# Final stage of a hybrid decoder step: PSUM as VectorE's work space, the norm's weights on GpSimd, the scaling on ScalarE

## The chip, the cores and the metric

The kernel runs on one core of one Trainium2 chip. The metric is device time in microseconds (us) of one execution; the median of 3 runs counts. A core has TensorE for matmuls (PE in the profile), VectorE (DVE), ScalarE (ACT), GpSimd (POOL) and SyncE (SP), which issues most DMAs. SBUF and PSUM are its two on-chip memories, both of 128 partitions; PSUM has 8 banks of 512 float32 per partition.

## The reference, cut to what matters

The reference is one layer of a decoder for 1024 prompt tokens and 8 sample tokens (D_MODEL 1024, float32): an mLSTM and a convolution, then a mixture of experts (top 2 of 32), a residual add and a final RMSNorm. The change is about the last lines only:

```
out = out + jnp.einsum('nef,efd->nd', hid * combine[:, sl, None], w_down[sl])   # two experts per token
...
x = x + g2[:, None] * moe
...
y_prompt = rms_norm(xp, final_g)
y_sample = rms_norm(xs, final_g)
```

`rms_norm` is `xf * rsqrt(mean(xf * xf) + EPS) * g`.

## The kernel before, in words

The 1032 tokens are 9 tiles: tiles 0 to 7 hold 128 prompt tokens each, tile 8 the 8 sample tokens. Each engine has its own program, and the order on an engine is written out by hand; between engines semaphores are waited on (`sem(name)` counters; a DMA adds 16). `chain(...)` on an engine makes its next instruction wait for the one just issued.

The experts run one after the other (32, and in this run 4 more passes for experts with more than 128 tokens; `nq` counts such groups of four). TensorE multiplies, ScalarE and VectorE split every float32 weight into a high and a low part (`ehi`, `elo`, `dhi`, `dlo`), GpSimd gathers tokens and scatters each expert's results to `ye_dram` (named `expert_results` in the trace), where row 2t+c is the c-th expert's result for token t. SP loads the weights of an expert into one of 4 slots of `eraw` and `draw`, as slots come free (`gu_ps` counts the gate-and-up products done). The residual stream lies in `x2_dram` (`x_scratch` in the trace).

The final stage begins when VectorE has seen all scatters land (`experts_done`, line 1383). Its buffers `xf` (residual), `y12` (the two expert results of each token) and `of` (output) lie where the expert weights were. `xf` and `y12` have FB = 4 places, `of` has 2, so a tile's loads wait for an earlier tile's place. For each tile:

- ScalarE, `weighted` (line 1189): first result times its weight, in place in `y12`.
- VectorE, lines 1399, 1400, 1402: second result times its weight plus the first; times `g2b` (the gate g2); plus the residual, into `xf`.
- ScalarE, lines 1200 to 1202: squares of `xf`, summed into `ssq`; logarithm; exponential, which gives 1/rms.
- VectorE, `scaled` (line 1391): `xf` times 1/rms times `fgb` (final_g), into `of`. It is issued one tile later, after the next tile's three passes.
- SP, `y_out` (line 1049): stores the tile. SP also loads: the first four residual tiles once the last expert's gate-and-up product is done (line 1027), the first four `y12` tiles after `experts_done`, and each later tile behind the store of the tile four before it.

Of the kernel before, what the change touches and what calls it, by code (L numbers as in the profile page):

```python
# [104 lines left out]
def build(nc, x_prompt, x_sample, c_prompt, c_sample, C0, n0, m0, cache, w_ada, b_ada, norm1_g, w_in,  # L105
# [10 lines left out]
    with ExitStack() as ctx:  # L116
        sems = {}

        def sem(name):
            if name not in sems:  # L120
                sems[name] = ctx.enter_context(nc.semaphore(name))
            return sems[name]

        def step(name):

            return sem("steps_" + STEP[name][0])
# [15 lines left out]
        def sb(scope, name, shape, dt=F32):  # L142
            return scope.enter_context(nc.sbuf_tensor(name, shape, dt))
# [851 lines left out]
        def moe_loads(sp):  # L995
            sp.wait_ge(sem("h2_ready"), NT)
            for e in range(NS):
                gate_up_load(sp, e, e, None)
                down_load(sp, e, e, None)
            sp.dma_start(fgb[:, :], final_g.rearrange("(o n) -> o n", o=1).broadcast_to([P, D])).then_inc(sem("fg_in"), 16)  # L1000
            for e in range(NS, NE):
                gate_up_load(sp, e, e % NS, e - NS + 1)
                if e > NS:
                    down_load(sp, e - 1, (e - 1) % NS, e - NS)
            down_load(sp, NE - 1, NS - 1, NE - NS)

            sp.wait_ge(step("nov_ready"), after("nov_ready"))
            nq = sp.value_load(nov[0:1, 0:1], min_val=0, max_val=MORE)
            with sp.Fori(QUADS, QUADS + MORE) as r:
                with sp.If(nq + QUADS > r):  # L1010
                    for half in range(2):
                        es = [sp.value_load(ovx[0:1, bass.ds(r * NS + (2 * half + b - NE), 1)], min_val=0, max_val=NE - 1)
                              for b in range(2)]
                        for b in range(2):
                            q = 2 * half + b
                            gate_up_load(sp, es[b], q, r * NS + (q - NS + 1))
                        for b in range(2):
                            q = 2 * half + b
# [12 lines left out]
            for t in range(NT + FB - 1):
                if t < NT:
                    b, m = t % FB, rows[t]
                    if t >= FB:
                        sp.wait_ge(sem("of_ready"), t - FB + 1)
                        x2_load(t)

                    sp.dma_start(y12[0:m, b, :, :].rearrange("p c n -> p (c n)"),
                                 ye_dram[2 * t * P:2 * (t * P + m), :].rearrange("(t c) n -> t (c n)", c=2))\
                      .then_inc(sem(f"y12_in{b}"), 16)  # L1040
                if t >= FB - 1:
                    y_out(sp, t - FB + 1)
            for s, v in (("out_done", 16 * 2), ("tails_out", 32), ("m_out", 32), ("c_out", 64), ("state_out", 32), ("x2_out1", 16 * 4),
                         ("h2_out", 16 * NT), ("y_out0", 16 * 5), ("y_out1", 16 * 4)):
                sp.wait_ge(sem(s), v)

        def y_out(sp, t):
            sp.wait_ge(sem("of_ready"), t + 1)
            sp.dma_start(y_d[t], of[0:rows[t], t % 2, :]).then_inc(sem(f"y_out{t % 2}"), 16)

        def moe_pool(pool, chain):
            pool.wait_ge(step("stage1_over"), after("stage1_over"))
# [44 lines left out]
                        late_scatter(r * NS + (q - LATE), (q - LATE) % 2, passes, r * 32 + 16 * ((q - LATE) // 2))  # L1097
            for q in range(LATE):
                late_scatter(nq * NS + (NE - LATE + q), (q - LATE) % 2, nq * (2 * NS) + 2 * q, nq * 32 + 16 * ((NE - LATE + q) // 2))

        def moe_act(act, chain):
            act.wait_ge(step("gmax_ready"), after("gmax_ready"))
# [82 lines left out]
            def weighted(t):  # L1185

                b, m = t % FB, rows[t]
                act.wait_ge(sem(f"y12_in{b}"), 16 * (t // FB + 1))
                act.activation(y12[0:m, b, 0, :], y12[0:m, b, 0, :], ACT.Copy, scale=wts[0:m, 0, t:t + 1])\
                   .then_inc(sem("ya_ready"), 1)  # L1190

            weighted(0)
            for t in range(NT):
                if t + 1 < NT:
                    weighted(t + 1)
                b, m = t % 2, rows[t]
                act.wait_ge(sem("xsum_ready"), t + 1)
                if t >= 2:
                    act.wait_ge(sem(f"y_out{b}"), 16 * (t // 2))
                chain(act.activation(of[0:m, b, :], xf[0:m, t % FB, :], ACT.Square, accum_out=ssq[0:m, b, 0:1]))  # L1200
                chain(act.activation(ssq[0:m, b, 1:2], ssq[0:m, b, 0:1], ACT.Ln, bias=epst[0:m, :], scale=1.0 / D))
                act.activation(ssq[0:m, b, 1:2], ssq[0:m, b, 1:2], ACT.Exp, scale=-0.5).then_inc(sem("rf_ready"), 1)

        def moe_dve(dve, chain):
            def signal(name):
# [181 lines left out]
            def scaled(t):

                m, b = rows[t], t % 2
                dve.wait_ge(sem("rf_ready"), t + 1)  # L1390
                dve.scalar_tensor_tensor(out=of[0:m, b, :], in0=xf[0:m, t % FB, :], scalar=ssq[0:m, b, 1:2], in1=fgb[0:m, :],  # L1391
                                         op0=ALU.mult, op1=ALU.mult).then_inc(sem("of_ready"), 1)


            for t in range(NT):
                b, m = t % FB, rows[t]
                dve.wait_ge(sem("ya_ready"), t + 1)
                ya, yb = y12[0:m, b, 0, :], y12[0:m, b, 1, :]
                chain(dve.scalar_tensor_tensor(out=ya, in0=yb, scalar=wts[0:m, 1, t:t + 1], in1=ya, op0=ALU.mult, op1=ALU.add))  # L1399
                chain(dve.tensor_tensor(ya, ya, g2b[0:m, t // NC_, :], ALU.mult))  # L1400
                dve.wait_ge(sem(f"xf_in{b}"), 16 * (t // FB + 1))
                dve.tensor_tensor(xf[0:m, b, :], xf[0:m, b, :], ya, ALU.add).then_inc(sem("xsum_ready"), 1)  # L1402
                if t:
                    scaled(t - 1)
            scaled(NT - 1)
# [644 lines left out]
```

## Time and profile before

| | us |
|---|---|
| median of 3 runs | 1085.94 (1085.92 to 1086.76) |
| profiled execution, its own time | 1092.49 |
| its span, first to last instruction | 1089.5 |
| busy in the span: TensorE / VectorE / ScalarE / GpSimd | 941.8 / 750.1 / 493.5 / 156.3 |
| `experts_done` in the span | 1035.97 |

Busy times are averages over stages with different limits. The change is read from the last stage alone, the stretch from 1035.97 to 1089.5, 53.5 us, in which TensorE does nothing. All times of day below count from the span's start.

### The profile page before, as it was taken

The numbers are of one execution on the slowest core, as the hardware profiler recorded it, in microseconds if no ns is written. First come the engines' busy times: TensorE is split into PE (matmuls) and PEld (weight loads), VectorE is DVE, ScalarE is ACT, GpSimd is POOL, SyncE is SP. The second block draws the span as 40 slices with busy tenths as digits, with TensorE's granted clock in tenths as the row PEclk, the third lists the DMA queues.
The fourth block names the chain that finished last, engine by engine and source line by source line (L and its number), as shares of the span: only waits on it lengthen the run. The fifth ranks groups of instructions, "written<-read, shape, count | busy, mean of one in ns | idle before, by whom it ended". The sixth has DMA issues, their size and how long they took to land. (4 is left out here: it accounts for less than half of the span.)

```text
span 1089.5 us, 12729 instructions
## 1 busy us (share of the span) xinstructions
PE 941.8 (86%) x4961; PEld 765.1 (70%) x4961; DVE 750.1 (69%) x939; ACT 493.5 (45%) x621; POOL 156.3 (14%) x120
## 2 busy tenths in 40 slices
PE   4599999989999989999999815899999999999700
PEld 2298979989999776666665314688888888888500
DVE  3441399969995343656445348799999999989478
ACT  4451212133121353333222204588888888888344
POOL 0100000000000000000000001133444444365200
PEclk9699999999999968899999956899999999999955
DMA  7963711102120160111141196489999999997276
GB/s 266 363 267 106 299 56 39 39 1 48 45 67 1 79 199 20 58 59 59 59 136 72 47 246 255 180 342 377 360 406 380 388 391 380 410 379 308 94 301 245
DMA packets 64775, 213.14 MB, mean 196 GB/s; under 512 B 13856, under 2 KB 34992, under 8 KB 46782
## 3 DMA queue, kind: packets, MB, share of 16 engines
q1 hardware_dynamic: 54350, 195.42, 47.9%
q0 software_dynamic: 10368, 16.93, 4.2%
q8 instruction: 39, 0.64, 0.2%
q14 instruction: 18, 0.15, 0.0%
HBM read 199.14 MB, written 34.49 MB: 214 GB/s over the span
## 5 line engine op out<-in xcount | busy, mean ns | idle before, releaser
L1220 DVE TENSOR_TENSOR elo<-eraw,ehi 128x2048 fp32r<-128x2048 f32 x72 | 161.4, 2283 | 0.0
L1846 DVE SCALAR_TENSOR_TENSOR z<-z,wdT 128x1024 f32<-128x1024 f32 x120 | 146.2, 1280 | 0.8
L1112 ACT ACTIVATE ehi<-eraw 128x2048 fp32r<-128x2048 f32 x72 | 133.6, 1907 | 1.9 <-issue 1.0
L1957 PE MATMUL ps<-hhi,whi 128*128 128x344 f32 x576 | 125.5, 327 | 6.4 <-ACT hhi L1690 3.6
L848 PE MATMUL ps<-wout,z 128*128 128x512 f32 (+1 forms) x288 | 127.6, 596 | 0.5 <-DVE z L688 0.5
L1957 PE MATMUL ps<-hhi,wlo 128*128 128x344 f32 x576 | 123.5, 323 | 0.0
L1957 PE MATMUL ps<-hlo,whi 128*128 128x344 f32 x576 | 122.9, 322 | 0.0
L1668 ACT ACTIVATE z<-ps 128x1032 f32<-128x1032 f32 x24 | 24.8, 1034 | 210.8 <-PE ps L1957 210.8
L1957 PEld LDWEIGHTS ps<-hhi,whi 128*128 128x128 f32 x576 | 98.6, 192 | 9.4 <-issue 9.3
L1957 PEld LDWEIGHTS ps<-hhi,wlo 128*128 128x128 f32 x576 | 98.7, 191 | 0.0
L1957 PEld LDWEIGHTS ps<-hlo,whi 128*128 128x128 f32 x576 | 97.2, 190 | 0.0
L848 PEld LDWEIGHTS ps<-wout,z 128*128 128x128 f32 (+1 forms) x288 | 50.7, 181 | 64.7 <-issue 64.0
L1819 DVE TENSOR_TENSOR wlo<-wraw,whi 128x1024 fp32r<-128x1024 f32 x22 | 26.9, 1225 | 83.7 <-ACT whi L1662 83.6
L1225 DVE TENSOR_TENSOR dlo<-draw,dhi 128x2048 fp32r<-128x2048 f32 x36 | 82.4, 2288 | 0.0
L1430 PE MATMUL ps<-ehi,xhi 128*128 128x512 f32 x288 | 77.4, 411 | 2.1 <-issue 2.1
L1063 POOL DMA_INDIRECT expert_results<-ysb,lists x27 | 72.5, 2684 | 34.6 <-ACT ysb L1138 34.6
L1430 PE MATMUL ps<-ehi,xlo 128*128 128x512 f32 x288 | 72.7, 395 | 0.0
L1430 PE MATMUL ps<-elo,xhi 128*128 128x512 f32 x288 | 71.1, 389 | 0.0
L1118 ACT ACTIVATE dhi<-draw 128x2048 fp32r<-128x2048 f32 x36 | 69.6, 1932 | 0.0
L1053 POOL IOTA ioti<- 128x128 int32 x1 | 0.2, 240 | 472.0 <-DVE marks L1207 472.0
L1344 DVE TENSOR_TENSOR xlo<-ps,xhi 128x1024 fp32r<-128x1024 f32 x36 | 44.1, 1225 | 30.2 <-ACT xhi L1122 30.2
L1430 PEld LDWEIGHTS ps<-ehi,xlo 128*128 128x128 f32 x288 | 55.4, 192 | 12.0
(368 smaller groups left out, 1489.7 us busy)
## 6 DMA issues: line engine op xcount, KB each, us to landing
eraw<-in_w_gate SPq DMA_DIRECT2D x36, 1024.0 KB, 11.5
eraw<-in_w_up SPq DMA_DIRECT2D x36, 1024.0 KB, 14.5
draw<-in_w_down SPq DMA_DIRECT2D x36, 1024.0 KB, 14.7
wada<-in_w_ada SPq DMA_DIRECT2D x24, 1024.0 KB, 10.5
wraw<-in_w_in SPq DMA_DIRECT2D x12, 1024.0 KB, 5.3
y<-expert_results SPq DMA_DIRECT2D x8, 1024.0 KB, 7.6
xt<-in_x_prompt SPq DMA_DIRECT2D x8, 512.0 KB, 6.2
wout<-in_w_out SPq DMA_DIRECT2D x2, 2048.0 KB, 10.0
```

Source lines behind the costliest of these rows:

```text
L848: mm = pe.matmul(ps[0:n, bank + a, :], lhs, wout[:, k, a * 512:(a + 1) * 512], start=(k == H), stop=(k == H - 1))
L1063: pool.indirect_dma_start(out=ye_dram, in_=ysb[:, b, :], in_offset=None, out_offset=bass.IndirectOffsetOnAxis(ap=at, axis=0), bounds_check ...
L1112: act.activation(ehi[:, s % 2, i, :, :], eraw[:, s, i, :, :], ACT.Copy).then_inc(sem("ehi_ready"), 1)
L1118: act.activation(dhi[:, s % 2, :, :], draw[:, s, :, :], ACT.Copy).then_inc(sem("dhi_ready"), 1)
L1220: dve.tensor_tensor(elo[:, s, i, :, :], eraw[:, s, i, :, :], ehi[:, s % 2, i, :, :].bitcast(F32), ALU.subtract)\
L1225: dve.tensor_tensor(dlo[:, s, :, :], draw[:, s, :, :], dhi[:, s % 2, :, :].bitcast(F32), ALU.subtract)\
L1344: dve.tensor_tensor(xlo[:, b, :, :], ps[:, 0:2, :].rearrange("p a (k n) -> p (a k) n", k=4), xhi[:, b, :, :].bitcast(F32), ALU.subtract).t ...
L1430: mm = pe.matmul(ps[:, 2, :].rearrange("p (i f) -> p i f", i=2), x[:, b, k, :], w[:, :, k, :], start=(i + k == 0), stop=(i == 2 and k == K ...
L1668: act.activation(z[:, j, PAD:ZW].rearrange("p (c n) -> p c n", c=3), ps[:, 3 * v:3 * v + 3, 0:TW], ACT.Sigmoid if GB0 <= j < Q0 or j >= O0 ...
L1819: dve.tensor_tensor(wlo[:, u, :, v * P:(v + 1) * P], wraw[:, u, :, v * P:(v + 1) * P], whi[:, v, :, :].bitcast(F32), ALU.subtract).then_in ...
L1846: dve.scalar_tensor_tensor(out=z[:, GB0 + b, PAD:SC], in0=z[:, U0 + b, w:w + T], scalar=wdT[:, b, w:w + 1], in1=z[:, GB0 + b, PAD:SC], op0 ...
L1957: mm = pe.matmul(ps[0:n, bank + c, 0:TW], w(k), h[:, k, c * TW:(c + 1) * TW], start=first, stop=last)
```

## The change

The final stage is written anew; the experts' arithmetic stays.

- ScalarE writes the weighted first result into PSUM instead of SBUF. VectorE's first two passes read and write it there, and the third adds it to the residual in SBUF. Four pairs of banks are used in turn.
- The product with `fgb` moves to GpSimd (`of` = `xf` times `fgb`), and the product with 1/rms to ScalarE, in place in `of`, one tile later. VectorE keeps both for the last tile only.
- `xf`, `y12` and `of` get a place for each tile, so no load or store waits for a place.
- The residual is loaded within the last experts: tiles 0 to 3, 4 to 7 and 8 when the first, second and third slot of the last group of experts are done with.
- The sample tile comes first (`FINAL`). Six loads bring `y12`: tile 8, tile 0, tile 1, then tiles 2 and 3, 4 and 5, 6 and 7 (`GROUP`).

```
-FB = 4
+FINAL = (8, 0, 1, 2, 3, 4, 5, 6, 7)
+GROUP = (1, 2, 3, 3, 4, 4, 5, 5, 0)
...
-        xf = sb(st3, "xf", [P, FB, D])
-        y12 = sb(st3, "y12", [P, FB, 2, D])
-        of = sb(st3, "of", [P, 2, D])
+        xf = sb(st3, "xf", [P, NT, D])
+        y12 = sb(st3, "y12", [P, NT, 2, D])
+        of = sb(st3, "of", [P, NT, D])
...
+            sp.wait_ge(sem("gu_ps"), nq * NS + (NE - NS + 1))
+            x2_load(range(4))
+            sp.wait_ge(sem("gu_ps"), nq * NS + (NE - NS + 2))
+            x2_load(range(4, 8))
+            sp.wait_ge(sem("gu_ps"), nq * NS + (NE - NS + 3))
+            x2_load((8,))
             sp.wait_ge(step("experts_done"), after("experts_done"))
...
+            for g in range(max(GROUP) + 1):
+                y12_load(g)
+            for i, t in enumerate(FINAL):
+                if i == NT - 1:
+                    sp.wait_ge(sem("of_last"), 1)
+                else:
+                    sp.wait_ge(sem("of_ready"), i + 1)
+                sp.dma_start(y_d[t], of[0:rows[t], t, :]).then_inc(sem("y_out"), 16)
...
+            pool.wait_ge(sem("fg_in"), 16)
+            pool.wait_ge(step("experts_done"), after("experts_done"))
+            for i, t in enumerate(FINAL[:-1]):
+                m = rows[t]
+                pool.wait_ge(sem("xsum_ready"), i + 1)
+                pool.tensor_tensor(of[0:m, t, :], xf[0:m, t, :], fgb[0:m, :], ALU.mult).then_inc(sem("fgx_ready"), 1)
...
+            def weighted(i):
...
+                if i >= 4:
+                    act.wait_ge(sem("xsum_ready"), i - 3)
+                act.activation(ps[0:m, 2 * b:2 * b + 2, :].rearrange("p a n -> p (a n)"), y12[0:m, t, 0, :], ACT.Copy,
+                               scale=wts[0:m, 0, t:t + 1]).then_inc(sem("ya_ready"), 1)
+
+            def scaled(i):
...
+                act.wait_ge(sem("fgx_ready"), i + 1)
+                act.activation(of[0:m, t, :], of[0:m, t, :], ACT.Copy, scale=ssq[0:m, b, 1:2]).then_inc(sem("of_ready"), 1)
...
+            for i, t in enumerate(FINAL):
+                m, b = rows[t], i % 4
+                y = ps[0:m, 2 * b:2 * b + 2, :].rearrange("p a n -> p (a n)")
+                dve.wait_ge(sem("ya_ready"), i + 1)
+                chain(dve.scalar_tensor_tensor(out=y, in0=y12[0:m, t, 1, :], scalar=wts[0:m, 1, t:t + 1], in1=y, op0=ALU.mult, op1=ALU.add))
+                chain(dve.tensor_tensor(y, y, g2b[0:m, t // NC_, :], ALU.mult))
+                dve.tensor_tensor(xf[0:m, t, :], xf[0:m, t, :], y, ALU.add).then_inc(sem("xsum_ready"), 1)
```

What stands in a row on ScalarE for one tile in the middle of the stage, before (each row: line, operation, output and inputs, partitions by elements, the semaphores waited for):

```order
L1189 ACTIVATE y12<-y12,wts 128x1024 [waits y12_in1]
L1200 ACTIVATE of,ssq<-xf 128x1024 [waits y_out0,xsum_ready]
L1201 ACTIVATE ssq<-ssq,epst 128x1 [waits act_chain]
L1202 ACTIVATE ssq<-ssq 128x1 [waits act_chain]
L1189 ACTIVATE y12<-y12,wts 128x1024 [waits y12_in2]
```

And of the changed kernel, from the weighting of one tile to that of the next:

```order
L1203 ACTIVATE ps<-y12,wts 128x1024 [waits xsum_ready,y12_in4]
L1219 ACTIVATE y12,ssq<-xf 128x1024 [waits xsum_ready]
L1220 ACTIVATE ssq<-ssq,epst 128x1 [waits act_chain]
L1221 ACTIVATE ssq<-ssq 128x1 [waits act_chain]
L1211 ACTIVATE of<-of,ssq 128x1024 [waits fgx_ready]
L1203 ACTIVATE ps<-y12,wts 128x1024 [waits xsum_ready,y12_in5]
```

A second pass over the tile (line 1211) now stands between the exponential and the next weighting, and the Square no longer waits for a store (`y_out0`).

VectorE at the end of its program, before:

```order
L1400 TENSOR_TENSOR y12<-y12,g2b 8x1024 [waits dve_chain]
L1402 TENSOR_TENSOR xf<-xf,y12 8x1024 [waits xf_in0,dve_chain]
L1391 SCALAR_TENSOR_TENSOR of<-xf,ssq,fgb 128x1024 [waits rf_ready]
L1391 SCALAR_TENSOR_TENSOR of<-xf,ssq,fgb 8x1024 [waits rf_ready]
L116 UNCONDITIONAL_BRANCH
```

And of the changed kernel:

```order
L1415 TENSOR_TENSOR xf<-xf,ps 128x1024 [waits dve_chain]
L1413 SCALAR_TENSOR_TENSOR ps<-y12,wts,ps 128x1024 [waits ya_ready]
L1414 TENSOR_TENSOR ps<-ps,g2b 128x1024 [waits dve_chain]
L1415 TENSOR_TENSOR xf<-xf,ps 128x1024 [waits dve_chain]
L1418 SCALAR_TENSOR_TENSOR of<-xf,ssq,fgb 128x1024 [waits rf_ready]
```

Three passes per tile follow each other with one scaling at the very end, of a full tile; before it was the 8-row tile that came last.

SP's DMAs around `experts_done` (the wait on `steps_DVE`), before:

```order
L992 DMA draw<-in_w_down 128x2048 [waits down_ps] x2
...
L1023 DMA xf<-x2_scratch 128x1024 [waits gu_ps]
L1023 DMA xf<-x2_scratch 128x1024 x3
L1038 DMA y12<-expert_results 128x2048 [waits steps_DVE]
L1038 DMA y12<-expert_results 128x2048 x3
L1049 DMA out_0<-of 128x1024 [waits of_ready]
L1023 DMA xf<-x2_scratch 128x1024 [waits of_ready]
```

And of the changed kernel:

```order
L993 DMA draw<-in_w_down 128x2048 [waits down_ps] x2
...
L1024 DMA xf<-x2_scratch 128x1024 [waits gu_ps]
L1024 DMA xf<-x2_scratch 128x1024 x3
...
L1024 DMA xf<-x2_scratch 8x1024 [waits gu_ps]
L1040 DMA y12<-expert_results 8x2048 [waits steps_DVE]
L1040 DMA y12<-expert_results 128x2048 x2
L1040 DMA y12<-expert_results 128x2x2048 x3
L1051 DMA out_1<-of 8x1024 [waits of_ready]
L1051 DMA out_0<-of 128x1024 [waits of_ready] x7
L1051 DMA out_0<-of 128x1024 [waits of_last]
```

All residual loads now stand behind the last weights and ahead of `experts_done`, and the stores behind all loads (tiles 4 to 7 of the residual, a second row of four loads, read like the first).

## Rows read from the trace of the kernel before

**Rows 1.** Windows view: length, busy per engine, TensorE's granted clock, DMA share, GB/s.
```profile
1056.00:1066.00 10.00, 0.00 (x0) 0.00 (x0) 9.86 (x9) 4.89 (x8) 0.00 (x0) 0.50 1.01 392
```

**Rows 2.** Groups by line, 1041 to 1089.5: busy us, mean ns, idle before.
```profile
L1391 DVE SCALAR_TENSOR_TENSOR of<-xf,ssq,fgb 128x1024 f32<-128x1024 f32 (+1 forms) x9 | 11.5, 1276 | 0.6 <-ACT ssq L1202 0.6
L1189 ACT ACTIVATE y<-y,wts 128x1024 f32<-128x1024 f32 (+1 forms) x9 | 10.3, 1143 | 13.8 <-DMA y<-expert_results 13.8
```

**Rows 3.** Timeline of one tile in mid-stage: start us, duration us, engine, line.
```profile
1048.35 1.23 DVE L1402 TENSOR_TENSOR xf<-xf,y 128x1024 f32<-128x1024 f32 x1
1049.49 1.28 DVE L1391 SCALAR_TENSOR_TENSOR of<-xf,ssq,fgb 128x1024 f32<-128x1024 f32 x1
1049.61 1.06 ACT L1200 ACTIVATE of<-xf 128x1024 f32<-128x1024 f32 x1 [0.96 <-DVE xf L1402]
...
1050.69 1.28 DVE L1399 SCALAR_TENSOR_TENSOR y<-y,wts 128x1024 f32<-128x1024 f32 x1
...
1051.12 0.20 ACT L1202 ACTIVATE ssq<-ssq 128x1 f32<-128x1 f32 x1
...
1051.22 1.13 ACT L1189 ACTIVATE y<-y,wts 128x1024 f32<-128x1024 f32 x1
...
1054.40 1.28 DVE L1391 SCALAR_TENSOR_TENSOR of<-xf,ssq,fgb 128x1024 f32<-128x1024 f32 x1
```

**Rows 4.** Timeline of the stage's start (SPq is SP's issue of DMAs).
```profile
1036.06 1.93 SPq L1038 DMA_DIRECT2D y<-expert_results  x4
1040.77 1.15 ACT L1189 ACTIVATE y<-y,wts 128x1024 f32<-128x1024 f32 x1 [3.43 <-DMA y<-expert_results]
1042.06 1.28 DVE L1399 SCALAR_TENSOR_TENSOR y<-y,wts 128x1024 f32<-128x1024 f32 x1 [6.03 <-ACT y L1189]
```

**Rows 5.** The end: timeline, waits of SP's queue, landing of the last 512 KB store.
```profile
1085.32 2.15 SPq L1049 DMA_DIRECT2D out<-of  x2
...
1085.87 1.27 DVE L1391 SCALAR_TENSOR_TENSOR of<-xf,ssq,fgb 8x1024 f32<-8x1024 f32 x1 [0.58 <-ACT ssq L1202]
...
SPq L1045 <- DMA out<-of: 1.3, 1, 1.3
...
DMA to landing us min/median/max: 2.6/2.6/2.6
```

**Rows 6.** PSUM operands elsewhere in the kernel: two timeline rows, one group by line.
```profile
427.79 1.23 DVE L615 TENSOR_TENSOR ps<-ps,bcv 128x1024 f32<-128x1024 f32 x1 [6.35 <-PE ps L848]
429.05 1.22 DVE L617 TENSOR_TENSOR x<-x,ps 128x1024 f32<-128x1024 f32 x1
...
L1138 ACT ACTIVATE ysb<-ps 128x1024 f32<-128x1024 f32 x36 | 37.3, 1036 | 2.7 <-PE ps L1450 2.7
```

**Rows 7.** Timelines of VectorE and GpSimd in the experts, in pairs that overlap.
```profile
994.07 2.29 DVE L1225 TENSOR_TENSOR dlo<-draw,dhi 128x2048 fp32r<-128x2048 f32 x1
...
994.60 1.79 POOL L1080 COPY scur<-lists 128x1 int32 x1
...
1008.14 0.41 DVE L1355 TENSOR_TENSOR tlo<-ps,thi 128x256 fp32r<-128x256 f32 x1
...
1008.25 0.18 POOL L1083 TENSOR_TENSOR passed<-ones 1x1 f32<-1x1 f32 x1 [4.21 <-ACT ysb L1138]
```

**Rows 8.** Timelines near 45 us: GpSimd's only large two-input passes, VectorE beside them.
```profile
45.26 4.66 POOL L1614 TENSOR_TENSOR wlo<-wraw,whi 128x1024 fp32r<-128x1024 f32 x2 [42.45 <-ACT whi L1662]
...
44.75 1.20 DVE L1777 COPY hf<-ps 128x1024 f32<-128x1024 f32 x1
```

**Rows 9.** Windows view, columns as in the first group.
```profile
1005.00:1024.00 19.00, 16.90 (x73) 13.74 (x72) 10.58 (x8) 8.12 (x10) 5.59 (x6) 0.91 0.02 7
1038.00:1040.00 2.00, 0.00 (x0) 0.00 (x0) 0.00 (x0) 0.00 (x0) 0.00 (x0) 0.50 0.99 414
```

**Rows 10.** Timeline of SP's queue in the last experts.
```profile
985.52 9.62 SPq L992 DMA_DIRECT2D draw<-in_w_down  x2
1023.77 1.75 SPq L1023 DMA_DIRECT2D xf<-x_scratch  x4
```

More of the change, by code:

```diff
@@ L1019, in moe_loads, with x2_load @@
                             down_load(sp, es[b], q, r * NS + (q - NS + 1))
-            def x2_load(t):
-                b, m = t % FB, rows[t]
-                sp.dma_start(xf[0:m, b, :], x2_dram[t * P:t * P + m, :]).then_inc(sem(f"xf_in{b}"), 16)
+            def x2_load(tiles):
+                for t in tiles:
+                    sp.dma_start(xf[0:rows[t], t, :], x2_dram[t * P:t * P + rows[t], :]).then_inc(sem("xf_in"), 16)
             for b in range(2):
                 sp.wait_ge(sem(f"x2_out{b}"), 16 * (5 - b))
-            sp.wait_ge(sem("gu_ps"), nq * NS + NE)
@@ L1028, in moe_loads @@
-            for t in range(FB):
-                x2_load(t)
-            sp.wait_ge(step("experts_done"), after("experts_done"))
[L1031 to L1042, printed above, removed]
+            sp.wait_ge(sem("gu_ps"), nq * NS + (NE - NS + 1))
@@ new lines, in moe_loads, with y12_load @@
+            x2_load(range(4))
[3 more added lines that the diff above has]
+            x2_load((8,))
+            sp.wait_ge(step("experts_done"), after("experts_done"))
+            def y12_load(g):
+                mine = [t for t in range(NT) if GROUP[t] == g]
+                t, m = mine[0], rows[mine[0]]
+                sp.dma_start(y12[0:m, t:t + len(mine), :, :].rearrange("p b c n -> p b (c n)"),
+                             ye_dram[2 * t * P:2 * (t * P + m * len(mine)), :].rearrange("(b t c) n -> t b (c n)", c=2, t=m))\
+                  .then_inc(sem(f"y12_in{g}"), 16)
@@ L1043, in moe_loads @@
+            for g in range(max(GROUP) + 1):
[6 more added lines that the diff above has]
+                sp.dma_start(y_d[t], of[0:rows[t], t, :]).then_inc(sem("y_out"), 16)
             for s, v in (("out_done", 16 * 2), ("tails_out", 32), ("m_out", 32), ("c_out", 64), ("state_out", 32), ("x2_out1", 16 * 4),
[L1044 removed]
+                         ("h2_out", 16 * NT), ("y_out", 16 * NT)):
@@ L1045, in moe_loads @@
                 sp.wait_ge(sem(s), v)
-        def y_out(sp, t):
-            sp.wait_ge(sem("of_ready"), t + 1)
-            sp.dma_start(y_d[t], of[0:rows[t], t % 2, :]).then_inc(sem(f"y_out{t % 2}"), 16)
         def moe_pool(pool, chain):
@@ L1183, in moe_act @@
             act.preload_act_table_set(LNEXP)
[L1185 to L1190, printed above, removed]
-            weighted(0)
[L1193 to L1200, printed above, removed]
+            def weighted(i):
+                t, b = FINAL[i], i % 4
+                m = rows[t]
+                act.wait_ge(sem(f"y12_in{GROUP[t]}"), 16)
+                if i >= 4:
[3 more added lines that the diff above has]
+            def scaled(i):
+                t, b = FINAL[i], i % 2
+                m = rows[t]
+                act.wait_ge(sem("fgx_ready"), i + 1)
+                act.activation(of[0:m, t, :], of[0:m, t, :], ACT.Copy, scale=ssq[0:m, b, 1:2]).then_inc(sem("of_ready"), 1)
+            weighted(0)
+            for i, t in enumerate(FINAL):
+                if i + 1 < NT:
+                    weighted(i + 1)
+                b, m = i % 2, rows[t]
+                act.wait_ge(sem("xsum_ready"), i + 1)
+                chain(act.activation(y12[0:m, t, 0, :], xf[0:m, t, :], ACT.Square, accum_out=ssq[0:m, b, 0:1]))
                 chain(act.activation(ssq[0:m, b, 1:2], ssq[0:m, b, 0:1], ACT.Ln, bias=epst[0:m, :], scale=1.0 / D))
                 act.activation(ssq[0:m, b, 1:2], ssq[0:m, b, 1:2], ACT.Exp, scale=-0.5).then_inc(sem("rf_ready"), 1)
+                if i:
+                    scaled(i - 1)
         def moe_dve(dve, chain):
@@ L1385, in moe_dve @@
             dve.wait_ge(sem("fg_in"), 16)
[L1387 to L1405, printed above, removed]
+            dve.wait_ge(sem("xf_in"), 16 * NT)
+            for i, t in enumerate(FINAL):
+                m, b = rows[t], i % 4
[4 more added lines that the diff above has]
+                dve.tensor_tensor(xf[0:m, t, :], xf[0:m, t, :], y, ALU.add).then_inc(sem("xsum_ready"), 1)
+            t, m, b = FINAL[-1], rows[FINAL[-1]], (NT - 1) % 2
+            dve.wait_ge(sem("rf_ready"), NT)
+            dve.scalar_tensor_tensor(out=of[0:m, t, :], in0=xf[0:m, t, :], scalar=ssq[0:m, b, 1:2], in1=fgb[0:m, :],
+                                     op0=ALU.mult, op1=ALU.mult).then_inc(sem("of_last"), 1)
         def moe_pe(pe):
```

## The prediction

> **What bounds the kernel now.** The chain of work that ended last runs, from the moment the experts are done, through one wait for a load and then through VectorE alone, so I read the final stage by itself: first its windows, then its groups by line, then one tile row by row. In ten microseconds of mid-stage VectorE is busy for 9.86 and ScalarE for 4.89, GpSimd and TensorE not at all [rows 1]. The DMA engines are as busy as VectorE there, and ScalarE waits 13.8 us for the expert results [rows 2]; but those are waits of an engine that has time, since VectorE's own rows touch each other. One tile takes VectorE 4.91 us, from one scaling at 1049.49 to the next at 1054.40 [rows 3]: 1.20 for the scaling (to 1050.69) and 3.71 for the three passes. Nine tiles at 4.91 are 44.2; VectorE starts at 1042.06 and the last scaling ends at 1085.87 + 1.27 = 1087.14 [rows 4, 5], 45.1 us. The rest is the end of the last norm, where VectorE waits 0.6 [rows 2]. So the stage is 4.7 us of load (1036.06 to 1040.77), 1.3 of the first weighting, 45.1 of VectorE, and 2.4 from its last end to the end of the span, 1089.5.
>
> **What it removes from VectorE.** Eight of the nine scalings (11.5 us for nine, [rows 2]); 3.71 us a tile remain. VectorE's passes through PSUM: the kernel already has the second and third pass in just this form, PSUM in and out at 1.23 us and PSUM added to SBUF at 1.22, with 1.26 from start to start [rows 6]. I take the first pass at its 1.28 [rows 3] too. Nothing gained, nothing lost; the bound on either side is a hundredth per pass.
>
> **What it adds to ScalarE.** Per tile, one more pass, priced as the weighting, 1.13 [rows 3], also with a scale for each partition. The weighting itself now writes to PSUM, which no row shows. The nearest rows: it takes 1.14 in SBUF, and a copy from PSUM 1.04 [rows 2, 6]. I keep 1.14, and allow 0.1 either way. The Trainium skill (ScalarE: Activation LUTs, Step-by-step: what each stage is for) says that ScalarE writes faster to PSUM than to SBUF; no run here shows it, and by it the time would be a little below mine.
>
> ScalarE's own round per tile: from Square to the next instruction 1.61 (1049.61 to 1051.22), and two passes that overlap the next by 0.10 (the exponential ends at 1051.32 when the weighting has begun at 1051.22), 1.03 each [rows 3]: 3.67 us, just under VectorE's 3.71. But neither runs freely, because a weighting is issued only one tile ahead. The loop is: weighting to VectorE's first pass 1.29 (1040.77 to 1042.06, [rows 4]); first pass to third pass 2.57 (3.71 less the 1.14 of the third, which starts at 1048.35 and is followed at 1049.49); third pass to Square 1.26 (1048.35 to 1049.61); Square to scaling 1.61; scaling to the next weighting 1.03 [rows 3]. That is 7.76 us for a loop that moves on by two tiles, so **3.88 us per tile**: the larger of 3.67, 3.71 and 3.88.
>
> **GpSimd.** Its only comparable pass, two inputs from SBUF of 128x1024, took 4.66 for two, 2.33 each [rows 8]. It starts when a tile's sum is there, and ScalarE wants the product one tile plus a Square chain later, 3.88 + 1.61 = 5.49 us: 3 us of slack, and 2.33 is below 3.88, so it costs nothing. If that cover went, it would be paid on ScalarE's path. It could still cost VectorE time. The experts show that the two engines can hold each other up: a one-column copy on GpSimd, issued 0.5 us into a VectorE subtraction of two SBUF tensors, took 1.79 us and ended at 996.39, with the subtraction (996.36), while a tiny operation beside a subtraction of PSUM and SBUF took 0.18 [rows 7]. And at 45 us the first large GpSimd pass began 0.7 us before a VectorE copy out of PSUM ended; both passes together took 4.66, the copy 1.20 [rows 8]. After the change every VectorE pass that runs beside GpSimd has one input in PSUM. By these rows the price is nothing; the other end is that they exclude each other, a rival below. The Trainium skill (SBUF — State Buffer, Who interferes with whom) says the same: a VectorE instruction with two SBUF inputs contends with a GpSimd instruction that reads SBUF, one with at most one SBUF input, outside VectorE's two-port modes, does not. By that rule the sum has no term for GpSimd; by a lock that took every VectorE pass it would have the rival's.
>
> **The loads.** The residual's 4.2 MB move into a stretch with room: from 1005 to 1024 the DMA engines are busy for 0.02, and they move 414 GB/s when nothing stops them [rows 9], so 10.2 us are needed. They stand behind the last weights in SP's queue, whose issue ends at 995.14 [rows 10], and ahead of nothing but `experts_done`. The loads at 1023.77 that they replace are gone from beside the last scatters. I take nothing for either.
>
> The expert results come at 414 GB/s, 2.53 us for a tile of 1 MB, and a tile is used in 3.88; the 64 KB tile goes first. Its landing is shown nowhere: a 1 MB tile lands 4.71 after issue [rows 4], a 32 KB store 1.6 after (VectorE ends at 1087.14, issue at 1087.47, then 1.3 of waiting: 1088.8, [rows 5]). I take 2.3, near the small one because of its size. Tile 0 lands some 0.5 later than before, about 1041.3, since its issue is second; the fourth tile in turn, which shares a load with the fifth, lands near 1041.3 + 3 x 2.53 = 1048.9 and is weighted at about 1049.8. That is the tightest place, with 0.9 us to spare; a delay there moves everything behind it.
>
> **The sum.** First weighting 1036.06 + 2.3 = 1038.36; VectorE on the sample tile at 1039.65; on tile 0 at 1043.36 (its data would allow 1042.6); seven more tiles at 3.88: tile 7 begins at 1070.52. Its third pass and the step to ScalarE take 2.57 + 1.26: Square at 1074.35. The exponential ends 1051.32 - 1049.61 = 1.71 later [rows 3], and VectorE's last scaling takes 1.28: 1077.34. The end is dearer than before: tile 6's store is issued only when ScalarE has scaled it, 1074.35 + 1.61 + 1.14 = 1077.1, and tile 7's 512 KB stands behind it. One such store lands in 2.6 [rows 5], the second 1.27 later at 414 GB/s: 1081.0. From the last landing to the end there were 0.7 (1088.8 to 1089.5). So the span ends at **1081.7, 7.8 us less than 1089.5**. The profiled execution took 1092.49 in its own time, 6.55 above the median; I take the gain over unchanged: 1085.94 - 7.8 = **1078.1 us**.
>
> Bounds: the small load at 1.6 or 4.7 gives -0.7 or +2.4; the PSUM write moves the loop by 0.1 in two tiles, 0.4 in all; stores that don't queue -1.3; a pitch of VectorE alone (3.71) -1.2. Together about 1075 to 1081.
>
> **Rivals.** *GpSimd and VectorE exclude each other after all* (slower). Each multiply then holds VectorE up for 2.33, VectorE's tile is 6.04, 2.16 above 3.88, and eight of them are 17.3 us: 1095.4. It turns the change into a loss once VectorE loses more than about 1 us per tile (7.8 over 8). Against it stand rows 7 and 8; for it, that no row shows a large pass with one SBUF input beside a large GpSimd pass.
>
> *ScalarE is slower than priced.* If its passes did not overlap, or the write to PSUM cost 0.3 more, the pitch would be near 4.3 and the gain 3 us less: 1081.4. For it, that loop and free rounds lie within 0.2 of each other, so any small wait shows.
>
> *The loads bite.* If the residual's transfers delay the last weights or scatters, up to 10.2 us come back before `experts_done`: 1088.3 at worst, 1080 at a likely 2. Against it: the queue's order and the idle stretch.
>
> *Nothing happens*, because the stage was bound by transfers: expert results and stores are 12.6 MB, 30.6 us at 414 GB/s, so they would end near 1068, ahead of 1081. I give this little.
>
> **How the numbers follow.** Forecast (a gain of 5 to 10.5 us) 0.78; ScalarE slower or loads late, a gain of 2.2 to 5, 0.11; nothing 0.04; slower 0.07, most of it the lock. 0.2%, 2.2 us, is about what a measurement of this kernel can tell from no change; so faster 0.89, same 0.04, slower 0.07. The range runs from 1075.3, the sum of the favourable bounds, to 1081.6, the unfavourable ones and the slower ScalarE.
>
> **What would show it.** Right: VectorE's three passes at 1.2 to 1.3 us with gaps of about 0.1 to 0.2 per tile, waiting for ScalarE's weighting; Squares 3.9 us apart; GpSimd's eight passes near 2.33; `experts_done` at about 1036; no DMA wait on ScalarE after the second tile; two stores in flight at the end. Wrong: VectorE or GpSimd passes stretched while they overlap, residual loads that push `experts_done` later, or a weighting that waits for tiles 2 and 3.

## The result, and the profile after

The changed kernel took 1075.3 us, the median of four runs (1071.52, 1071.98, 1078.61 and 1079.19), beside 1086.35 for the kernel before in the same comparison (1085.92 to 1091.94, four runs). The ratio is 0.9897, 95% interval 0.9866 to 0.9929. It is faster, with a gain of 11.1 us where 7.8 was forecast. The median lies on the low bound of the range, 1075.3; the gain lies outside it, since that bound stood for 10.6 us (1085.94 - 1075.3). Two executions of the kernel before, of 1353.69 and 2104.77 us, lie far from all others and are left out of every median and range below.

The profiled execution took 1071.52 us, its span 1069.7, against 1092.49 and 1089.5 before. First the page of the changed kernel: the busy line of each engine, and the clock granted to TensorE in 40 slices.

```profile
PE 929.9 (87%) x4961; PEld 754.1 (70%) x4961; DVE 740.6 (69%) x931; ACT 501.0 (47%) x629; POOL 175.1 (16%) x128
PEclk9899999999999979999999956899999999999965
```

Then its timeline: the mark at the end of the first part of the program (629.33), the mark `experts_done` and the stage's start, a tile in mid-stage, and the end. The columns are start, duration, engine, line and operation, and in brackets the idle time before it and what ended it.

```profile
629.33 0.06 DVE L1228 MEMSET marks<- 1x1 f32 x1 [7.83 <-DMA out<-caug]
...
1024.51 0.06 DVE L1404 MEMSET marks<- 1x1 f32 x1 [8.40 <-DMA expert_results<-ysb,scur]
1024.60 3.01 SPq L1040 DMA_DIRECT2D y<-expert_results  x6
1027.09 1.11 ACT L1203 ACTIVATE ps<-y,wts 8x1024 f32<-8x1024 f32 x1 [1.21 <-DMA y<-expert_results]
1028.34 1.28 DVE L1413 SCALAR_TENSOR_TENSOR ps<-y,wts,ps 8x1024 f32<-8x1024 f32 x1 [3.77 <-ACT ps L1203]
...
1032.29 2.35 POOL L1110 TENSOR_TENSOR of<-xf,fgb 8x1024 f32<-8x1024 f32 x1 [10.21 <-DVE xf L1415]
...
1043.38 1.29 DVE L1413 SCALAR_TENSOR_TENSOR ps<-y,wts,ps 128x1024 f32<-128x1024 f32 x1
1043.49 1.06 ACT L1219 ACTIVATE y<-xf 128x1024 f32<-128x1024 f32 x1 [0.15 <-DVE xf L1415]
1043.54 2.35 POOL L1110 TENSOR_TENSOR of<-xf,fgb 128x1024 f32<-128x1024 f32 x1 [1.55 <-DVE xf L1415]
1044.70 1.23 DVE L1414 TENSOR_TENSOR ps<-ps,g2b 128x1024 f32<-128x1024 f32 x1
1045.11 1.13 ACT L1211 ACTIVATE of<-of,ssq 128x1024 f32<-128x1024 f32 x1
1045.97 1.22 DVE L1415 TENSOR_TENSOR xf<-xf,ps 128x1024 f32<-128x1024 f32 x1
1046.15 1.10 ACT L1203 ACTIVATE ps<-y,wts 128x1024 f32<-128x1024 f32 x1
1047.22 1.06 ACT L1219 ACTIVATE y<-xf 128x1024 f32<-128x1024 f32 x1
1047.28 1.29 DVE L1413 SCALAR_TENSOR_TENSOR ps<-y,wts,ps 128x1024 f32<-128x1024 f32 x1
...
1051.12 1.06 ACT L1219 ACTIVATE y<-xf 128x1024 f32<-128x1024 f32 x1 [0.15 <-DVE xf L1415]
...
1062.49 1.06 ACT L1219 ACTIVATE y<-xf 128x1024 f32<-128x1024 f32 x1 [0.98 <-DVE xf L1415]
1064.10 1.13 ACT L1211 ACTIVATE of<-of,ssq 128x1024 f32<-128x1024 f32 x1
1064.23 1.29 DVE L1418 SCALAR_TENSOR_TENSOR of<-xf,ssq,fgb 128x1024 f32<-128x1024 f32 x1 [1.78 <-ACT ssq L1221]
```

Where a full tile took VectorE 4.91 us with four passes [rows 3], it now takes three, at 1.29, 1.23 and 1.22. Two tiles apart, the Squares stand 7.63 us apart (1043.49 and 1051.12), 3.82 per tile. GpSimd's pass lies beside VectorE's first and second passes without stretching either. In ten microseconds of mid-stage VectorE is still busy nearly throughout, and now ScalarE is too; the row before had 4.89 for ScalarE and 0.00 for GpSimd [rows 1]. The windows view, with the columns of [rows 1]: the length, the busy time of TensorE, of its weight loads, of VectorE, ScalarE and GpSimd, then the granted clock, the DMA share and GB/s (the other three rows are used below):

```profile
251.45:286.42 34.97, 34.97 (x231) 34.85 (x230) 34.48 (x34) 8.48 (x10) 0.00 (x0) 1.00 0.28 61
431.21:479.73 48.52, 47.68 (x204) 29.30 (x203) 29.51 (x76) 16.72 (x50) 0.00 (x0) 0.97 0.18 66
629.33:1024.51 395.18, 354.73 (x1728) 296.35 (x1728) 342.47 (x361) 289.04 (x257) 147.97 (x100) 0.94 0.87 341
1040.00:1050.00 10.00, 0.00 (x0) 0.00 (x0) 9.70 (x9) 9.66 (x18) 6.70 (x3) 0.50 0.95 377
```

**The gain has two parts.** The final stage, from `experts_done` to the end of the span, is 1069.7 - 1024.51 = 45.2 us. The kernel before had its two marks here, in its own timeline:

```profile
638.20 0.06 DVE L1207 MEMSET marks<- 1x1 f32 x1 [8.20 <-DMA out<-caug]
...
1035.97 0.06 DVE L1383 MEMSET marks<- 1x1 f32 x1 [8.40 <-DMA expert_results<-ysb,scur]
```

Its final stage was 1089.5 - 1035.97 = 53.5 us, so the stage gained **8.3**. But the two spans differ by 19.8, and 11.5 us of that lie ahead of `experts_done`. Of these, 8.9 lie ahead of the first mark, in stages that the diff does not touch, and 2.6 in the experts, where it moves only the residual loads. The windows of the kernel before for the same three sections (between the same marks), and for two short stretches in the second:

```profile
253.17:289.66 36.49, 36.49 (x231) 36.37 (x230) 34.47 (x34) 8.48 (x10) 0.00 (x0) 0.95 0.27 59
437.06:489.92 52.86, 52.02 (x215) 32.58 (x215) 29.60 (x75) 17.05 (x51) 0.00 (x0) 0.93 0.16 60
...
453.00:457.00 4.00, 4.00 (x25) 2.74 (x23) 3.69 (x9) 2.80 (x8) 0.00 (x0) 1.00 0.28 114
461.00:465.00 4.00, 4.00 (x19) 3.64 (x18) 2.75 (x11) 2.39 (x6) 0.00 (x0) 0.53 0.00 0
...
638.20:1035.97 397.77, 357.56 (x1728) 298.33 (x1728) 342.53 (x361) 289.01 (x257) 148.02 (x100) 0.94 0.85 334
```

Each section was slower before by 1.5, 4.3 and 2.6 us. In the first two the clock granted to TensorE was lower on average (0.95 and 0.93 against 1.00 and 0.97), with TensorE busy for 98% of the section or more. The short stretches show what such a mean is made of: full clock (2.4 GHz) at 453 to 457, nearly the lower level (1.2 GHz) at 461 to 465, though TensorE was busy in all of both. In the third section the clock is 0.94 in both kernels, and TensorE was busy 2.8 us longer before (357.56 and 354.73). VectorE and ScalarE did the same work in the same busy time, to within 0.4.

### The profile page after: what moved, and what is told of

Read it like the earlier page. It is cut to its first block and busy times, and to the rows that moved or that the text cites. A ratio compares the mean times of both kernels' runs of the same rounds, so it can differ in the third digit from the quotient of the medians.

```text
span 1069.7 us, 12727 instructions
## 1 busy us (share of the span) xinstructions
PE 929.9 (87%) x4961; PEld 754.1 (70%) x4961; DVE 740.6 (69%) x931; ACT 501.0 (47%) x629; POOL 175.1 (16%) x128
## 5 line engine op out<-in xcount | busy, mean ns | idle before, releaser
L1063 POOL DMA_INDIRECT xg<-h_scratch,glists x32 | 34.4, 1073 | 171.0 <-PE ps L1431 131.4
## 6 DMA issues: line engine op xcount, KB each, us to landing
wada<-in_w_ada SPq DMA_DIRECT2D x24, 1024.0 KB, 10.3
```

The source lines that it names most:

```text
L1063: pool.indirect_dma_start(out=xg[:, b, :], out_offset=None, in_=h2_dram, in_offset=bass.IndirectOffsetOnAxis(ap=at, axis=0), bounds_check= ...
```

## The experiments

Two theories stood at the start. A: the final stage went as predicted, and the rest of the difference is spread from execution to execution, of the clock of TensorE ahead of the stage. B: the change itself makes the part ahead shorter. Beside these stand rivals for single terms. Every kernel here computes the whole reference.

**Both kernels again, unchanged**, the first two side by side, the third later.

> The kernel before, unchanged, for its spread. The profiled execution of before reached experts_done at 1035.97 us, that of the changed kernel at 1024.51, and 8.9 of these 11.5 us lie ahead of the experts, which the change doesn't touch. Theory A (TensorE's granted clock varies from one execution to the next in the stages ahead): the times of this kernel fall into levels some 7 us apart, the spans go with the mean granted clock, and experts_done lies anywhere from 1024 to 1036 while the final stage stays at 53.4 us. Theory B (the change shortened the part ahead): experts_done of this kernel stays at 1030 us or later in all executions, and the spread is below 2 us but for single ones.

> The changed kernel, unchanged, for its spread. Theory A: the same levels as the kernel before, shifted by the 8.3 us that the final stage lost in the two profiles (53.4 to 45.1 us), so a ratio near 0.9925. Theory B: experts_done stays near 1024 us, and the ratio is near 0.987, as in the first comparison (0.9897) or below.

> The changed kernel again, unchanged, to pool its times. Theory A (the final stage is 8.3 us shorter, the rest of the difference is TensorE's clock in the part ahead, which both kernels share): final stage 45.1 to 45.3 us, experts_done anywhere from 1024 to 1036, ratio to before near 0.9925. Theory B (the part ahead is shorter by another 3 us or more on average): ratio near 0.989 or below.

| run | time, median (range) | kernel before, measured beside it | ratio, 95% interval | span profiled | `experts_done` | final stage |
|---|---|---|---|---|---|---|
| before again | 1087.27 (1085.44 to 1091.13) | 1089.6 | 0.999, 0.9972 to 1.0009 | 1084.7 | 1031.19 | 53.5 |
| after again | 1079.15 (1076.36 to 1080.75) | 1089.6 | 0.991, 0.9886 to 0.9935 | 1075.7 | 1030.36 | 45.3 |
| after, third | 1077.68 (1073.65 to 1079.82) | 1087.99 | 0.9909, 0.9873 to 0.9944 | 1073.4 | 1028.20 | 45.2 |

The stage repeats within 0.1 us in each kernel, while `experts_done` of one and the same kernel moves by 5 us and more (1035.97 and 1031.19; 1024.51, 1030.36 and 1028.20). The same three sections in the second profile of the kernel before, and then the second of them in a later experiment that holds the whole change (the one with weighting ahead and single loads, below):

```profile
254.15:289.11 34.96, 34.96 (x231) 34.84 (x230) 34.48 (x35) 8.49 (x10) 0.00 (x0) 1.00 0.29 61
437.27:485.78 48.51, 47.67 (x206) 29.30 (x205) 29.51 (x76) 16.71 (x50) 0.00 (x0) 0.97 0.18 66
635.80:1031.19 395.39, 354.89 (x1728) 296.21 (x1728) 342.51 (x361) 289.20 (x257) 148.07 (x100) 0.94 0.86 336
```

```profile
433.43:486.29 52.86, 52.02 (x215) 32.48 (x214) 29.59 (x75) 17.11 (x51) 0.00 (x0) 0.93 0.16 60
```

The kernel before alone has the first section at 36.49 and 34.96, the second at 52.86 and 48.51, the third at 397.77 and 395.39. The changed kernel has the second at 48.52, and kernels with the change have it at 52.86 too. Over all 13 profiles it is near 48.5 (five times), 51.3 (five) or 52.9 (three), with a granted clock of 0.97 to 0.98 for the short and 0.93 for both long ones. Which of them an execution gets is therefore not a matter of the change. This supports A for the sections that differ most. I had expected the times to fall on levels some 7 us apart; they don't, as several such sections add up.

B is not excluded for a smaller amount, and the numbers lean to it. Over ten profiles with the code of the experts as changed, `experts_done` came at 1024.51 to 1033.62, and the two of the kernel before lie at 1031.19 and 1035.97. Three ratios, 0.9897, 0.991 and 0.9909, are gains of 11.2, 9.8 and 9.9 us. The stage's 8.3 alone would be 0.9924, which lies in the upper part of each of the three intervals. Taken together, 43 executions of the kernel before have a mean of 1088.2 us and 16 of the changed kernel one of 1077.4: 10.8 us, 2.5 more than the stage gives. If the executions are taken as independent, the standard error of that difference is 0.8 us.

**The weighted sum stays in SBUF.** All else is as in the changed kernel.

```diff
-                act.activation(ps[0:m, 2 * b:2 * b + 2, :].rearrange("p a n -> p (a n)"), y12[0:m, t, 0, :], ACT.Copy,
+                act.activation(y12[0:m, t, 0, :], y12[0:m, t, 0, :], ACT.Copy,
...
-                y = ps[0:m, 2 * b:2 * b + 2, :].rearrange("p a n -> p (a n)")
+                y = y12[0:m, t, 0, :]
```

> The changed kernel, but with the weighted sum kept in SBUF, so that all three VectorE passes have two SBUF inputs while GpSimd multiplies. Theory L (VectorE passes with two SBUF inputs and GpSimd passes that read SBUF exclude each other): every GpSimd pass of 2.35 us holds VectorE up or waits for it, VectorE's tile goes from 3.7 to about 6 us, the final stage from 45.1 to about 60 us. Rival (no contention, PSUM was not needed): passes of 1.22 to 1.28 us as before, the stage at 45.1 to 45.5 us.

The final stage is 61.0 us (1028.14 to 1089.1), the single time 1091.45. One tile in its timeline:

```profile
1047.29 1.28 DVE L1413 SCALAR_TENSOR_TENSOR y<-y,wts 128x1024 f32<-128x1024 f32 x1
...
1047.45 3.33 POOL L1110 TENSOR_TENSOR of<-xf,fgb 128x1024 f32<-128x1024 f32 x1 [2.42 <-DVE xf L1415]
...
1048.60 3.26 DVE L1414 TENSOR_TENSOR y<-y,g2b 128x1024 f32<-128x1024 f32 x1
...
1051.90 1.23 DVE L1415 TENSOR_TENSOR xf<-xf,y 128x1024 f32<-128x1024 f32 x1
1053.04 1.28 DVE L1413 SCALAR_TENSOR_TENSOR y<-y,wts 128x1024 f32<-128x1024 f32 x1
```

GpSimd's pass starts 0.16 us after VectorE's first pass and ends at 1050.78, 2.21 after that pass ends; it takes 3.33 instead of 2.35. VectorE's second pass, started meanwhile, ends 1.08 after GpSimd's (1051.86) and takes 3.26 instead of 1.23. Read by these ends, the two engines take turns, either waiting for the other, and the tile is 5.75 us (1047.29 to 1053.04). The predicted rival was real, with a price of 15.8 us for the stage, and PSUM is what keeps it away. The edit takes one input and the output of the first two passes out of PSUM together; which of the two counts, it does not show. For the input speaks that VectorE's subtraction of [rows 7] that reads PSUM and writes SBUF left a tiny GpSimd operation at 0.18. The Trainium skill (SBUF — State Buffer, Who interferes with whom) states that a VectorE instruction with two SBUF inputs contends with a GpSimd instruction that reads SBUF; the runs agree, 61.0 us with two SBUF inputs and 45.2 with one.

**VectorE does all the scalings**, as before the change; GpSimd's multiplies and ScalarE's scalings are taken out (not shown), the rest of the change stays.

```diff
...
+                if i:
+                    t, m, b = FINAL[i - 1], rows[FINAL[i - 1]], (i - 1) % 2
+                    dve.wait_ge(sem("rf_ready"), i)
+                    dve.scalar_tensor_tensor(out=of[0:m, t, :], in0=xf[0:m, t, :], scalar=ssq[0:m, b, 1:2], in1=fgb[0:m, :],
+                                             op0=ALU.mult, op1=ALU.mult).then_inc(sem("of_ready"), 1)
```

> The changed kernel, but VectorE does all nine scalings again (one tile late, as in the kernel before), and GpSimd and ScalarE none. If the split of the scaling is what the change earned, the pitch goes from 3.82 back to 4.9 us per tile and the stage from 45.1 to about 53 us, so that order, places and early loads are worth about 0.5 us together. Rival (the loads and places were worth half of the gain): the stage is near 49 us.

The stage is 52.2 us, the single time 1087.6. Its timeline shows the pitch of before, 4.91 us (1050.07 to 1054.99 is 4.92):

```profile
1050.07 1.28 DVE L1411 SCALAR_TENSOR_TENSOR of<-xf,ssq,fgb 128x1024 f32<-128x1024 f32 x1
1051.27 1.28 DVE L1405 SCALAR_TENSOR_TENSOR ps<-y,wts,ps 128x1024 f32<-128x1024 f32 x1
1052.58 1.23 DVE L1406 TENSOR_TENSOR ps<-ps,g2b 128x1024 f32<-128x1024 f32 x1
1053.85 1.22 DVE L1407 TENSOR_TENSOR xf<-xf,ps 128x1024 f32<-128x1024 f32 x1
1054.99 1.28 DVE L1411 SCALAR_TENSOR_TENSOR of<-xf,ssq,fgb 128x1024 f32<-128x1024 f32 x1
```

So the split of the scaling is worth 7.0 of the 8.3 us, and the new order, the places and the loads together 1.3, where 0.5 was expected. Passes through PSUM by themselves save VectorE nothing.

**The sample tile last instead of first**, so that a 1 MB load opens the stage and the small store ends it.

```diff
-FINAL = (8, 0, 1, 2, 3, 4, 5, 6, 7)
-GROUP = (1, 2, 3, 3, 4, 4, 5, 5, 0)
+FINAL = (0, 1, 2, 3, 4, 5, 6, 7, 8)
+GROUP = (0, 1, 2, 2, 3, 3, 4, 4, 5)
```

> The changed kernel, with the sample tile last again (tiles 0 to 7, then 8; loads in that order). By the prediction's sum, the start loses: the first weighting waits for a 1 MB tile, 4.7 instead of 2.5 us after issue; the end gains: the last store is 32 KB with 2.4 us from VectorE's end to the span's end, against 4.2. Theory A: the two nearly cancel, the final stage at 45.1 to 45.9 us against 45.1 to 45.3. Rival (starting with the small tile is worth a whole wait): 47 us or more.

The stage is 46.5 us (1029.59 to 1076.1), the single time 1078.34: between the two theories. From its timeline, the first weighting and the last scaling:

```profile
1034.40 1.12 ACT L1203 ACTIVATE ps<-y,wts 128x1024 f32<-128x1024 f32 x1 [3.45 <-DMA y<-expert_results]
...
1071.55 1.27 DVE L1418 SCALAR_TENSOR_TENSOR of<-xf,ssq,fgb 8x1024 f32<-8x1024 f32 x1 [1.77 <-ACT ssq L1221]
```

The first weighting comes 4.81 us after `experts_done` (2.58 in the changed kernel), and the end 3.3 after VectorE's last (4.2): the likely reason, not tested, is that the small store still stands behind tile 7's 512 KB. Having the small tile first gains more at the start than it loses at the end, 1.3 in all, as much as the experiment above left for order, places and loads together.

**All nine residual loads after the last gate and up**, as late as the first four were before.

```diff
-            sp.wait_ge(sem("gu_ps"), nq * NS + (NE - NS + 1))
-            x2_load(range(4))
-            sp.wait_ge(sem("gu_ps"), nq * NS + (NE - NS + 2))
-            x2_load(range(4, 8))
-            sp.wait_ge(sem("gu_ps"), nq * NS + (NE - NS + 3))
-            x2_load((8,))
+            sp.wait_ge(sem("gu_ps"), nq * NS + NE)
+            x2_load(range(9))
```

> The changed kernel, with all nine residual loads issued only after the last gate-and-up product, as the first four were before. 4.2 MB at 414 GB/s are 10.2 us and have some 12 us until experts_done. Theory A (the loads are hidden either way): the final stage stays at 45.1 to 46 us, and the last scatter lands in 3.2 to 4 us. Rival (the early loads are what unloads the stage): the last scatters or the first expert results come late, and the stage or the wait before it grows by 2 us or more.

The stage stays at 45.2 us (single time 1079.71), but its beginning is later. The loads' issue, the last scatter's, and the mark that waits for it, in its timeline:

```profile
1016.05 4.75 SPq L1024 DMA_DIRECT2D xf<-x_scratch  x9
...
1024.83 1.00 POOL L1064 DMA_INDIRECT expert_results<-ysb,scur  x1 [0.52 <-issue]
...
1032.23 0.06 DVE L1400 MEMSET marks<- 1x1 f32 x1 [12.39 <-DMA expert_results<-ysb,scur]
```

VectorE waits 12.39 us for that scatter, in both other kernels 8.40. The rival was right: with nine places the loads must come early or they cost 4.0 us, and early they gain nothing over before.

**The weighting two tiles ahead** opens the loop of 7.76 us on which the pitch rested.

```diff
             weighted(0)
+            weighted(1)
             for i, t in enumerate(FINAL):
-                if i + 1 < NT:
-                    weighted(i + 1)
+                if i + 2 < NT:
+                    weighted(i + 2)
```

> The changed kernel, with the weighting issued two tiles ahead instead of one. Theory A (a loop over two tiles through weighting, VectorE and Square sets the pitch, 3.82 us): the loop opens, VectorE runs at its own 3.71 to 3.75 us per tile without gaps, and the stage shortens by 0.5 to 0.9 us. Rival (ScalarE's own time sets the pitch): it stays at 3.82 us, Square waits for nothing, and the stage stays within 0.2 us.

The stage is 45.0 us, the single time 1076.87: the pitch is theory A's, the length of the stage the rival's. Two rows of its timeline show why:

```profile
1043.13 1.12 ACT L1203 ACTIVATE ps<-y,wts 128x1024 f32<-128x1024 f32 x1 [2.22 <-DMA y<-expert_results]
...
1069.58 1.29 DVE L1419 SCALAR_TENSOR_TENSOR of<-xf,ssq,fgb 128x1024 f32<-128x1024 f32 x1 [2.18 <-ACT ssq L1222]
```

VectorE did run free, at 3.72 per tile. But a weighting that comes earlier meets the load that tiles 2 and 3 share: ScalarE stands 2.22 us, with Squares and scalings behind it, and with a round of 3.68 against VectorE's 3.72 it hardly catches up. What VectorE gained, its last scaling waits for (2.18 against 1.78).

**The same with tiles 2 and 3 loaded singly.**

```diff
-GROUP = (1, 2, 3, 3, 4, 4, 5, 5, 0)
+GROUP = (1, 2, 3, 4, 5, 5, 6, 6, 0)
```

> The changed kernel, with two edits only: the weighting two tiles ahead, and tiles 2 and 3 loaded by themselves. If the loop over two tiles was the pitch of the changed kernel and the shared load hid that when the weighting went ahead, the stage falls from 45.2 to 44.4 to 44.7 us. Rival (the load was not it): 45.0 us as with the weighting ahead alone.

The stage is 44.7 us, the single time 1075.8: as expected, 0.5 under the changed kernel. VectorE's first passes in its timeline, 3.72 us apart, where the changed kernel has 3.90 (1043.38 to 1047.28):

```profile
1044.33 1.28 DVE L1414 SCALAR_TENSOR_TENSOR ps<-y,wts,ps 128x1024 f32<-128x1024 f32 x1
...
1048.05 1.28 DVE L1414 SCALAR_TENSOR_TENSOR ps<-y,wts,ps 128x1024 f32<-128x1024 f32 x1
```

**Ahead, and the scaling before the Square**, to shorten the end.

```diff
                 act.wait_ge(sem("fgx_ready"), i + 1)
+                act.wait_ge(sem("rf_ready"), i + 1)
...
+                if i:
+                    scaled(i - 1)
                 b, m = i % 2, rows[t]
                 act.wait_ge(sem("xsum_ready"), i + 1)
...
-                if i:
-                    scaled(i - 1)
```

> The changed kernel, with the weighting two tiles ahead and the scaling of the tile before issued ahead of a tile's Square instead of behind it. Theory A: pitch 3.71 to 3.75 us as with the weighting ahead alone, and the last but one store leaves some 2.5 us earlier, so the last one no longer stands behind it: the stage at 43.0 to 43.7 us. Rival (the queueing of the last two stores costs nothing): as the weighting ahead alone, 44.3 to 44.6 us.

The stage is 45.1 us, the single time 1076.24; both theories missed it. ScalarE stood 2.23 us at the same shared load, and VectorE's last scaling waited 3.06.

**All three together**, with the last tile scaled and stored in two halves of its columns (the halves only shown here).

```diff
-            dve.scalar_tensor_tensor(out=of[0:m, t, :], in0=xf[0:m, t, :], scalar=ssq[0:m, b, 1:2], in1=fgb[0:m, :],
-                                     op0=ALU.mult, op1=ALU.mult).then_inc(sem("of_last"), 1)
+            for c in (slice(0, D // 2), slice(D // 2, D)):
+                dve.scalar_tensor_tensor(out=of[0:m, t, c], in0=xf[0:m, t, c], scalar=ssq[0:m, b, 1:2], in1=fgb[0:m, c],
+                                         op0=ALU.mult, op1=ALU.mult).then_inc(sem("of_last"), 1)
```

> The changed kernel, with the weighting two tiles ahead, the scaling of the tile before ahead of a tile's Square, tiles 2 and 3 of the expert results loaded by themselves (1 MB each instead of 2 MB together), and the last tile scaled and stored in two halves of its columns. If it was the shared load that held ScalarE back by 2.2 us in the two runs with the weighting ahead, VectorE's 3.71 us per tile set the pitch to the end, its last scaling waits 1.9 us instead of 3.1, and the final stage takes 43.0 to 43.8 us against 45.2. Rival (ScalarE, 3.68 us per tile, falls behind anyway): 44.3 us or more.

The stage is 43.2 us (1028.39 to 1071.6), as expected: 2.0 under the changed kernel and 10.3 under the one before. The median is 1074.9 us (1072.14 to 1077.38), ratio 0.9887 (0.9852 to 0.9921), beside 0.9909 (0.9873 to 0.9944) for the changed kernel measured beside it. The intervals overlap: in the trace the two stages differ, by the measured times they can't be told apart yet. The end in its timeline:

```profile
1067.64 1.42 DVE L1424 SCALAR_TENSOR_TENSOR of<-xf,ssq,fgb 128x512 f32<-128x512 f32 x2 [1.78 <-ACT ssq L1228]
1068.42 0.99 SPq L1050 DMA_DIRECT2D out<-of  x2
```

The first half's store is issued 0.78 us after the scaling begins, while VectorE works on the second half, and the span ends 2.5 after VectorE's last instruction, against 4.2.

## Why the prediction was wrong, and what of it was right

**The step that failed** is the last of the sum: "I take the gain over unchanged: 1085.94 - 7.8". It makes the gain of the final stage the gain of the whole program, and puts the part ahead of the stage at nothing, with no reason and no bound. The gain of the stage was nearly right: 7.8 forecast, 8.3 measured. The gain of the program was 11.1, so some 2.7 us of it lie ahead of the stage. What the runs showed there is a part that moves by itself: `experts_done` at 1024.51, 1030.36 and 1028.20 in one and the same changed kernel, at 1035.97 and 1031.19 in the kernel before. How much of the 2.7 us is this spread and how much comes with the change stays open.

The bounds were all bounds on the final stage, 46 us of 1078, while the 1036 us ahead counted as fixed; only the rival of the loads looked ahead of the stage, and only for a loss. The rows spoke against that ahead of time: the profiled execution lay 6.55 us above the median of three runs, with the same code, and the prediction named that number and set it aside. In all executions the kernel before took 1080.5 to 1093.4 us and the changed kernel 1071.5 to 1080.8, so a median of three or four can lie well off the middle, and a range of 6 us had no room for it. The low bound was also added up wrongly: the favourable bounds listed (-0.7, -0.4, -1.3 and -1.2) make -3.6, or 1074.5 us, where the prediction calls 1075.3 their sum. With 1074.5 the median would have lain inside, and the 2.7 us would still have no place in the sum.

The changed kernel's second and third medians, 1079.15 and 1077.68, lie inside the range, but with some luck: the kernel before stood at 1089.6 and 1087.99 beside them, 2 to 4 us above the base of the sum, and the gains were 10.45 and 10.31.

**VectorE: three passes, unstretched.** Right: 1.29, 1.23 and 1.22, as taken from [rows 3, 6].

**The loop of two tiles.** Right: 7.63 against 7.76, 3.82 per tile against 3.88. That the loop sets the pitch, and not VectorE, is shown by opening it: 3.72. ScalarE's own round of 3.68 lies close behind, as the prediction's free rounds of 3.67 and 3.71 said.

**The write to PSUM.** A hair cheaper: 1.09 to 1.12 us against the 1.14 taken. The Trainium skill (ScalarE: Activation LUTs, Step-by-step: what each stage is for) says that ScalarE writes faster to PSUM; these rows agree in direction, with a difference of 0.02 to 0.05.

**GpSimd costs nothing.** Right, 2.35 against 2.33, in the form in which the change does it. Had VectorE kept two SBUF inputs, the rival was the outcome: 61.0 us, 7.5 slower than before. Its predicted pitch of 6.04 (3.71 and 2.33) was measured at 5.75: VectorE lost 2.04 us per tile (5.75 - 3.71).

**The loads.** The small load: weighting 2.49 after issue (1024.60 to 1027.09) against 2.3. The residual: `experts_done` waits 8.40 in both kernels, so no price, as taken; as late as before it would have been 4.0. The tightest place was named rightly: in the changed kernel ScalarE waits for a DMA only twice, 2.8 us in all, but as soon as the weighting comes earlier, the load of tiles 2 and 3 stops it.

**The end.** 4.2 us after VectorE's last pass (1065.52 to 1069.7) against 4.36, with two stores in flight: ScalarE ends the scaling of tile 6 at 1065.23, VectorE that of tile 7 at 1065.52. From the issue of the loads to the end 45.1 against 45.6.

**Open.** Whether the change itself also shortens the part ahead, by 1 to 3 us on average, and by what. The executions taken together say that more than the stage's 8.3 is likely (10.8, standard error 0.8). But the three sections have long and short lengths in the kernel before alone. The first stretch of the program is the only one found where both profiles of the kernel before stand outside the others: its mark came at 253.17 and 254.15 us before, and at 251.10 to 253.00 in all eleven profiles with a change, in code that the diff does not touch. No run shows a cause for that.

## What to carry to other kernels

When VectorE bounds a stage, GpSimd can take a whole pass off it. Here that paid because VectorE's passes beside it had one input in PSUM; with both in SBUF the two took turns, and the stage got longer than before (61.0 us, against 53.5). Work out the loop through the engine that feeds the bound, as well as each engine's own round, and look behind the wait that is opened for the next one. Put the spread of the part that is not changed into the range: a profile 6.55 us off the median of the same kernel is a first sign of its size.

## What the runs showed that was not expected

- One section of unchanged code has several lengths, 48.5 us with a granted clock of 0.97 and 51.3 or 52.9 with 0.93, the shortest and the longest of them in both kernels: the clock falls for some microseconds in the midst of work, 1.00 before it, 0.53 in it, and TensorE busy in both stretches.
- GpSimd's multiply of 8 rows takes as long as of 128: 2.35 us.
- A scatter behind residual loads of 4.2 MB let `experts_done` come 7.4 us after its issue (1024.83 to 1032.23); in the changed kernel, where the loads are over by then, 4.0 us less of waiting.
